# Rotary embedding: the swap of 32-row halves by transfers inside SBUF instead of a permutation matmul

## The chip, the cores and the metric

The kernel runs on one core of one Trainium2 chip. The metric is the device time of one execution in microseconds (us), smaller is better; for the kernel before it is the median of 3 runs. One more execution was taken by the profiler, and every row below is from it. The engines have short names: PE is TensorE's matmul, PEld its weight load, DVE VectorE, ACT ScalarE, POOL GpSimd, SP SyncE; SPq and POOLq are the issuing of DMAs by those engines.

## The reference: what is computed

Two transformer-like blocks for 512 tokens of width 1024. The change lies in the attention of the first one: 8 heads, and for each head q and k of two 64-wide components (128 columns together) and a v of 128 columns. q and k are normalised over each 64 columns and turned by the rotary embedding:

```python
def rope(t, cos, sin):
    tf = t.astype(jnp.float32)
    t1, t2 = jnp.split(tf, 2, axis=-1)
    out = jnp.concatenate([t1 * cos - t2 * sin, t2 * cos + t1 * sin], axis=-1)
    return out.astype(t.dtype)
...
        q = rope(rmsnorm(q, q_norm_gain[i]), cos, sin)
        k = rope(rmsnorm(k, k_norm_gain[i]), cos, sin)
...
        s = jnp.einsum('bqhcd,bkhcd->bhcqk', qblk, k).astype(jnp.float32) * scale
...
        p = jax.nn.softmax(s, axis=-1)
        a = p[:, :, 0] - lam * p[:, :, 1]
        return jnp.einsum('bhqk,bkhe->bqhe', a.astype(v.dtype), v)
```

## The kernel before

Everything is held transposed: features on the 128 partitions, the 512 tokens along the free axis. All weights are cut into 226 units of 128 output features (128x1024, 512 KB). A unit is loaded into one of four slots of `w_raw` by SP; ACT makes `w_hi` (L828) and `w_lo` = -`w_raw` (L829); and a transfer that adds, issued by POOL (L440), puts `w_raw` onto `w_lo`, where the low part of the split then stands. When it has landed it raises `lo_in` of the slot, and that tells SP that the slot of `w_raw` may be filled again, and PE that the unit may be multiplied. A tile of output is 24 matmuls (8 steps of high times high, low times high, high times low: L471 to L473) into one of two banks `pg`. A reader of a bank raises `pg_free`; `evacuated(engine, name)` waits for that.

Each engine has one instruction stream, and the order of the work is the order in which the code is written. In the stretch that matters a loop over `h` from 0 to 9 handles for each pass the tiles k, q and v of head h, the softmax of head g = h-1, and the weighted values and output norm of head h-2. PE's order in a pass from h = 2 to 7 is: tile k; the turn of v (L638) and scores of the first two query blocks of head g (L603, L605); weighted values of h-2 (`py`, L650); tile q; `turn(g, 0)` and `turn(g, 1)` (transposes of the probabilities `pa`, L613); `kq_sums` of k; the sum of squares of the output of head h-2 (`ssq_o`, L665); scores of blocks 2 and 3; tile v; `kq_sums` of q; `turn(g, 2)`, `turn(g, 3)`. In pass 0 there is only the work of head 0, and in pass 1 no L650 and no L665.

`kq_sums` (L616 to L622) holds two products for k or q: `block_ones` times the squares into the bank `px` (L620), and the permutation `rotate` times `kq_raw` into the bank `py` (L622), which swaps the 32-row halves of each 64 rows and turns one sign. Each is issued as one instruction and shows as two matmuls in the profile.

ACT evacuates a tile k or q in `kq_out` (L971 squares, L972 scaled copy `kq_raw`). `head_root` (L977 Ln, which reads `px` and frees it, and L979 Exp) makes the inverse root `kq_rs`. ACT runs in its written order: after tile q it does `kq_out` of q, the copy of `turn(g, 0)` out of PSUM (L962), `head_root` of k, `head_root` of the output, the Exps of the softmax (L950).

DVE's order in a pass from h = 2 on is: two maxima (L1477) and `combine` of blocks 0 and 1 (L1483, L1230, L1227, the last writing `pa`); a copy; the scaling of the output `hid` by `kq_rs` (L1227); the maxima of blocks 2 and 3; `rope_step` of k; `combine` of blocks 2 and 3; `rope_step` of q; a copy of `turn(g, 3)`. `scores` wait for `roped`, `turn` waits for `combed`. `rope_step` is four operations of 128x512: `kq_raw` times cosines, `py` times sines, the sum, and the product with `kq_rs`.

SP loads units 24 and on in a loop of four (L420 to L424), each as soon as its `lo_in` says so.

Of the kernel before, what the change touches and what calls it, by code (L numbers as in the profile page):

```python
# [7 lines left out]
P = 128  # L8
T = 512
D = 1024  # L10
KT = D // P
HEADS = 8
# [14 lines left out]
RING = 4  # L27
# [5 lines left out]
ALU = mybir.AluOpType  # L33
# [99 lines left out]
def aux_order():  # L133

    x, y, s = [("stat", 1), "lam", "kt"], [], []
    for name in ("bt", ("er", 0), ("er", 1), "e", "y"):
        s += [(name, 0), (name, 1)]
    for h in range(HEADS + 2):
        g = h - 1
        if 0 <= g < HEADS:  # L140
            x.append(("vt", g))
            s += [("s", g, 0), ("s", g, 1)]
        if h >= 2:
            y.append(("pv", h - 2))
        if 0 <= g < HEADS:
            s += [("t", g, 0), ("t", g, 1)]
        if h < HEADS:
            x.append(("ssq_k", h))
            y.append(("rot_k", h))
        if h >= 2:  # L150
            x.append(("ssq_o", h - 2))
        if 0 <= g < HEADS:
            s += [("s", g, 2), ("s", g, 3)]
        if h < HEADS:
            x.append(("ssq_q", h))
            y.append(("rot_q", h))
        if 0 <= g < HEADS:
            s += [("t", g, 2), ("t", g, 3)]
    x += [("stat", 2), ("stat", 3)]
    for t in range(LRU_T):  # L160
        x.append(("rg", t))
        y.append(("ig", t))
    for j in range(PAIRS + 1):
        if j > 0:
            for i in (0, 2):
                s += [("p", j - 1, i), ("p", j - 1, i + 1), ("t2", j - 1, i), ("t2", j - 1, i + 1)]
            y.append(("pv2", j - 1))
        if j < PAIRS:
            x.append(("vt2", j))
    x += [("stat", n) for n in (4, 5, 6)]  # L170
    return x, y, s
# [8 lines left out]
def build(nc, weights, x_dram, consts, rope, masks, params, ssm_b, ssm_c, lru_w, out):  # L180
    with ExitStack() as ctx:
        def sb(name, shape, dt=F32, scope=ctx):
            return scope.enter_context(nc.sbuf_tensor(name, shape, dt))

        def sem(name):
            return ctx.enter_context(nc.semaphore(name))
# [18 lines left out]
        with ExitStack() as first:  # L205
            gates = sb("gates", [P, 16, T], scope=first)
            y5 = sb("y5", [P, SSM_T, T], scope=first)
            with ExitStack() as s:
                gt = sb("gt", [P, 2, LANE_T, STEP + 1, GRP], scope=s)
                toep = sb("toep", [P, 2 * LANE_T, P], scope=s)  # L210
                e_sb = sb("e_sb", [P, 2, LANE_T, P], scope=s)
                lane = sb("lane", [P, 24, LANE_T], scope=s)
                pw = sb("pw", [P, 2, STEP + 1, LANE_T], scope=s)
                m16 = sb("m16", [P, GRP], scope=s)
                skip = sb("skip", [P, SSM_T, GRP], scope=s)
            with ExitStack() as s:
                rtab = sb("rtab", [P, 2, T], scope=s)
                kq_raw = sb("kq_raw", [P, 2, T], scope=s)
                kq_rs = sb("kq_rs", [P, 3, T], scope=s)
                rope_a = sb("rope_a", [P, 2, T], scope=s)  # L220
                kk = sb("kk", [P, 2, T], scope=s)
                qq = sb("qq", [P, 2, T], scope=s)
                v_raw = sb("v_raw", [P, T], scope=s)
                vv = sb("vv", [P, 2, QB, P], scope=s)
                pr = sb("pr", [P, 2, 2, T], scope=s)
                pa = sb("pa", [P, 2, T], scope=s)
                pt = sb("pt", [P, QB, T], scope=s)
                soft = sb("soft", [P, 2, 8], scope=s)
            mix_hi = sb("mix_hi", [P, KT, T], F32R, scope=first)
            mix_lo = sb("mix_lo", [P, KT, T], F32R, scope=first)  # L230
# [85 lines left out]
            sem(n) for n in ("e_made", "g_made", "scanned", "states", "toep_zero", "kt_made"))  # L316
        u_out, u_in, k_out, k_in, y_out, y_in = (sem(n) for n in ("u_out", "u_in", "k_out", "k_in", "y_out", "y_in"))
        gelu_done = sem("gelu_done")
        act_c, dve_c = sem("act_c"), sem("dve_c")
        roped, maxed, combed, o_sq, o_done = (sem(n) for n in ("roped", "maxed", "combed", "o_sq", "o_done"))  # L320
        rs_k, rs_q, rs_o = sem("rs_k"), sem("rs_q"), sem("rs_o")
# [30 lines left out]
        def py_read(eng, name):  # L352
            eng.wait_ge(py_free, YUSE[name] + 1)
# [13 lines left out]
        def _(sp):  # L367
# [14 lines left out]
            def next_weights(u):  # L382
                sp.wait_ge(lo_in[u % RING], 16 * (u // RING))
                sp.dma_start(w_raw[:, u % RING], weights[u].rearrange("p (k m) -> p k m", k=KT))\
                    .then_inc(w_landed[u % RING], 16)
# [30 lines left out]

            for u in range(22, 24):
                next_weights(u)
            full = len(UNITS) // RING
            with sp.Fori(24 // RING, full) as r:  # L420
                for s in range(RING):

                    sp.wait_ge(lo_in[s], r * 16)
                    sp.dma_start(w_raw[:, s], weights[r * RING + s].rearrange("p (k m) -> p k m", k=KT))\  # L424
                        .then_inc(w_landed[s], 16)
            for u in range(full * RING, len(UNITS)):
                next_weights(u)
            for k in range(KT):

                sp.wait_ge(fin_pool if k % 2 else fin_done, k // 2 + 1)  # L430
                sp.dma_start(out[:, k], hid[:, k]).then_inc(stored, 16)
# [25 lines left out]
        def _(pe):  # L457
# [30 lines left out]
            def y_use(name):  # L488
                if YUSE[name] > 0:
                    pe.wait_ge(py_free, YUSE[name])  # L490
# [125 lines left out]
            def kq_sums(h, name, n):  # L616

                x_use(("ssq_" + name, h))
                evacuated(pe, (name, h))
                pe.matmul(px[:], block_ones, kq_sq[n], start=True, stop=True).then_inc(px_full, 1)  # L620
                y_use(("rot_" + name, h))
                pe.matmul(py[:], rotate, kq_raw[:, n], start=True, stop=True).then_inc(py_full, 1)  # L622

            def glu(m):
                tile(UNIT[("glu", m // 2)], TILE[("glu", m)], XH, XL, first_split=SPLIT["g"] if m == 0 else None,
# [576 lines left out]
        def _(dve):  # L1202
# [8 lines left out]
            def link(ins):  # L1211

                put(ins, dve_c)
# [9 lines left out]
            def tt_(out_, a, b, op=ALU.mult):  # L1223
                return dve.tensor_tensor(out_, a, b, op)  # L1224
# [272 lines left out]

            def rope_step(h, name, n, ready, dst):
                evacuated(dve, (name, h))
                tt_(rope_a[:, 0], kq_raw[:, n], rtab[:, 0])  # L1500
                dve.wait_ge(py_full, YUSE[("rot_" + name, h)] + 1)
                tt_(rope_a[:, 1], py[:], rtab[:, 1]).then_inc(py_free, 1)
                py_read(dve, ("rot_" + name, h))
                link(tt_(rope_a[:, 0], rope_a[:, 0], rope_a[:, 1], ALU.add))
                dve.wait_ge(ready, h + 1)
                put(tt_(dst[:, h % 2], rope_a[:, 0], kq_rs[:, n]), roped)

            dve.wait_ge(r_landed, 16)
            for h in range(HEADS + 2):
                g = h - 1  # L1510
                attends = 0 <= g < HEADS
                if attends:
                    maximum(("s", g, 0), P, 0, soft)
                    maximum(("s", g, 1), 2 * P, 1, soft)
                    combine(g, 0)
                    combine(g, 1)
                if h == HEADS:
                    for t in range(SSM_T):
                        split_lo(SPLIT["g"] + t, x_lo[:, t], y5[:, t], x_hi[:, t])
                if h == HEADS + 1:  # L1520

                    for m in range(SSM_T):
                        evacuated(dve, ("glu", m))
                        put(tt_(y5[:, m], y5[:, m], sqr[:, m % 2]), src_done)
                    for m in range(SSM_T):
                        split_lo(SPLIT["s"] + m, x_lo[:, 4 + m], y5[:, m], x_hi[:, 4 + m])
                if attends:
                    turned(g, 1)
                if h >= 2:
                    py_read(dve, ("pv", h - 2))  # L1530
                    dve.wait_ge(rs_o, h - 1)
                    put(stt(hid[:, h - 2], hid[:, h - 2], lam_t[:, 6:7], kq_rs[:, 2]), o_done)
                if attends:
                    maximum(("s", g, 2), 3 * P, 2, soft)
                    maximum(("s", g, 3), 4 * P, 3, soft)
                if h < HEADS:
                    rope_step(h, "k", 0, rs_k, kk)
                if attends:
                    combine(g, 2)
                    combine(g, 3)  # L1540
                if h < HEADS:
                    rope_step(h, "q", 1, rs_q, qq)
                if attends:
                    turned(g, 3)
# [307 lines left out]
```

## Time and profile before

| what | value |
|---|---|
| time, median of 3 runs (lowest, highest) | 1555.84 us (1555.11, 1560.37) |
| the profiled execution's own time | 1564.44 us |
| its span, first to last instruction | 1562.6 us |
| PE busy, DVE busy, ACT busy | 94%, 41%, 53% |
| mean granted clock of TensorE | 0.969 |
| the passes h = 0 to 9, from the first `kq_raw` on | 228.0 to about 477 us |

The span leaves out 1.8 us of launch and end. Busy shares are means over stages with different limits, and a busy PE is not a PE at its peak; what a change in one stage is worth must be read from that stage's own waits. Clock is a share of full speed: 1.00 is 2.4 GHz, 0.50 is 1.2 GHz.

### The profile page before, as it was taken

The page shows a single profiled execution, that of the slowest core. Times are in us where ns is not written, and L with a number is a line of the kernel's source. Part 1 is how long each engine was busy: PE and PEld are TensorE (multiplying, and loading weights), DVE is VectorE, ACT ScalarE, POOL GpSimd, SP SyncE. Part 2 cuts the span into 40 slices and gives each one's busy share as a digit, 9 for nine tenths or more (in the row PEclk, how much of TensorE's full clock was granted, in tenths as well). Part 3 has the DMA queues.
Part 4 walks back from the last instruction along what each step waited for, and adds up shares of the span by engine and source line. Part 5 has one row for each costly group of instructions (what it writes and reads, how often), then busy time and mean ns, then how long its engine had stood idle before and what let it go on. Part 6 is the DMA issues. An engine that isn't in the chain of part 4 may idle for free.

```text
span 1562.6 us, 18066 instructions
## 1 busy us (share of the span) xinstructions
PE 1465.7 (94%) x6650; PEld 1140.8 (73%) x6654; DVE 636.1 (41%) x1116; ACT 825.3 (53%) x1147; POOL 203.7 (13%) x235
## 2 busy tenths in 40 slices
PE   4988879999989999999999999999989999999994
PEld 2876757666657887888888887677766888888883
DVE  4874004455464344555415424656515210212124
ACT  5632055666665456666535546655557554535431
POOL 0111001000001111111111111111010111111111
PEclk9998589999999999999999999999999999999997
DMA  7996276435426987888888888655484898888861
GB/s 242 189 184 116 48 186 151 108 95 118 108 61 158 243 186 167 193 191 195 194 197 182 204 195 215 157 132 126 102 183 101 194 196 187 189 196 192 193 150 57
DMA packets 82402, 253.22 MB, mean 162 GB/s; under 512 B 19856, under 2 KB 21008, under 8 KB 82192
## 3 DMA queue, kind: packets, MB, share of 16 engines
q0 software_dynamic: 32544, 118.50, 41.4%
q1 hardware_dynamic: 49344, 130.47, 28.5%
q10 hardware_dynamic: 432, 3.15, 0.6%
q8 instruction: 53, 0.87, 0.2%
q14 instruction: 29, 0.24, 0.1%
HBM read 129.14 MB, written 4.46 MB: 85 GB/s over the span
## 4 chain that ended last, share of the span: by engine, by line
PE 84%; DVE 5%; DMA 5%; ACT 2%; SPq 1%; issue 1%; POOLq 0%; POOL 0%; DVEq 0%; ACTq 0%
PE pg L471 24%; PE pg L473 24%; PE pg L472 24%; PE ps L603 1%; PE py L650 1%; PE ps L581 1%; PE ps L576 1%; DMA w_lo<-w_raw 1%; DMA w_raw<-weights 1%; PE py L622 1%; PE px L620 1%; DMA pairs<-u_dram 1%; DVE x_lo L1224 1%; DMA k_dram<-rstd 1%; PE ps L727 1%
## 5 line engine op out<-in xcount | busy, mean ns | idle before, releaser
L471 PE MATMUL pg<-x_hi,w_hi 128*128 128x512 f32 x1232 | 496.5, 403 | 21.7 <-DVE x_lo L1224 10.6
L472 PE MATMUL pg<-x_lo,w_hi 128*128 128x512 f32 x1232 | 483.8, 393 | 0.0
L473 PE MATMUL pg<-x_hi,w_lo 128*128 128x512 f32 x1232 | 483.7, 393 | 0.0
L440 POOL DMA_DIRECT2D w_lo<-w_raw x226 | 195.0, 867 | 1308.2 <-ACT w_lo L829 1281.4
L828 ACT ACTIVATE w_hi<-w_raw 128x1024 fp32r<-128x1024 f32 x226 | 237.5, 1051 | 146.9 <-PE pg L473 107.5
L471 PEld LDWEIGHTS pg<-x_hi,w_hi 128*128 128x128 f32 x1232 | 233.9, 190 | 84.0 <-issue 20.4
L472 PEld LDWEIGHTS pg<-x_lo,w_hi 128*128 128x128 f32 x1232 | 234.3, 190 | 49.8 <-issue 3.4
L473 PEld LDWEIGHTS pg<-x_hi,w_lo 128*128 128x128 f32 x1232 | 233.7, 190 | 49.9
L829 ACT ACTIVATE w_lo<-w_raw 128x1024 fp32r<-128x1024 f32 x226 | 236.4, 1046 | 0.0
L471 PE MATMUL pg<-act_hi,w_hi 128*128 128x512 f32 x432 | 170.3, 394 | 0.7 <-DMA w_lo<-w_raw 0.7
L473 PE MATMUL pg<-act_hi,w_lo 128*128 128x512 f32 x432 | 170.2, 394 | 0.0
L472 PE MATMUL pg<-act_lo,w_hi 128*128 128x512 f32 x432 | 170.2, 394 | 0.0
L471 PEld LDWEIGHTS pg<-act_hi,w_hi 128*128 128x128 f32 x432 | 80.8, 187 | 21.2 <-DMA w_lo<-w_raw 1.2
L472 PEld LDWEIGHTS pg<-act_lo,w_hi 128*128 128x128 f32 x432 | 80.8, 187 | 20.0
L473 PEld LDWEIGHTS pg<-act_hi,w_lo 128*128 128x128 f32 x432 | 80.8, 187 | 19.9
L1224 DVE TENSOR_TENSOR pairs<-rel 128x512 f32<-128x512 f32 x32 | 22.2, 692 | 150.6 <-ACT rel L1188 150.6
L1224 DVE TENSOR_TENSOR cu<-pg,rstd 128x512 f32<-128x512 f32 x44 | 30.4, 692 | 118.7 <-PE pg L473 118.6
L1227 DVE SCALAR_TENSOR_TENSOR cnv<-cu,prm,cnv 128x511 f32<-128x511 f32 x88 | 66.1, 751 | 3.1
L1224 DVE TENSOR_TENSOR hid<-hid,pg 128x512 f32<-128x512 f32 x32 | 22.0, 687 | 109.3 <-PE pg L473 109.3
L1224 DVE TENSOR_TENSOR acc<-acc,pg 128x512 f32<-128x512 f32 x24 | 16.6, 690 | 105.0 <-PE pg L473 105.0
L1477 DVE TENSOR_REDUCE soft<-ps 128x2 f32<-128x256 f32 (+3 forms) x48 | 39.6, 824 | 41.7 <-PE ps L605 35.5
L1224 DVE TENSOR_TENSOR rope_a<-kq_raw,rtab 128x512 f32<-128x512 f32 x16 | 11.1, 691 | 89.3 <-ACT kq_raw L972 88.8
(236 smaller groups left out, 1457.4 us busy)
## 6 DMA issues: line engine op xcount, KB each, us to landing
w_raw<-weights SPq DMA_DIRECT2D x226, 512.0 KB, 4.5
w_lo<-w_raw POOLq DMA_DIRECT2D x226, 512.0 KB, 5.8
hid<-x SPq DMA_DIRECT2D x4, 512.0 KB, 5.6
hid<-x ACTq DMA_DIRECT2D x1, 2048.0 KB, 12.0
out<-hid SPq DMA_DIRECT2D x8, 256.0 KB, 2.0
u_dram<-hid SPq DMA_DIRECT2D x4, 256.0 KB, 7.7
pairs<-u_dram SPq DMA_DIRECT2D x8, 128.0 KB, 10.2
y_dram<-hid SPq DMA_DIRECT2D x8, 128.0 KB, 5.0
```

The lines of the kernel that those rows point to most:

```text
L440: pool.dma_start(w_lo[:, s], w_raw[:, s], accum_op=ALU.add).then_inc(lo_in[s], 16)
L471: pe.matmul(bank[:], wh, xh(k), start=n == 0, stop=False)
L472: pe.matmul(bank[:], wh, xl(k), start=False, stop=False)
L473: last = pe.matmul(bank[:], wl, xh(k), start=False, stop=n == len(ks) - 1)
L576: pe.matmul(banks[h][:, NCH * n:NCH * n + NCH], toep[:, 2 * n + h, :], u_rows[:, 2 * n + h, :], start=True, stop=False)
L581: last = pe.matmul(banks[h][:, NCH * n + 1:NCH * n + NCH], gt[rows, r, n, 1:STEP + 1, :].rearrange("p d c -> p (d c)"), v_m[rows, r, n, 0: ...
L603: pe.matmul(bank[:, c, 0:w], qq[r, h % 2, P * i:P * i + P], kk[r, h % 2, 0:w], start=True, stop=False)
L828: act.activation(w_hi[:, s], w_raw[:, s], ACT.Copy)
L829: put(act.activation(w_lo[:, s], w_raw[:, s], ACT.Copy, scale=-1.0), hi_done)
L1224: return dve.tensor_tensor(out_, a, b, op)
L1227: return dve.scalar_tensor_tensor(out_, a, s, b, op0, op1)
L1477: put(dve.tensor_reduce(s[:, i % 2, 0:2], bank[:, :, 0:w], AX.X, ALU.max, negate=True), maxed)
```

## The change

The 16 products with `rotate` are gone. In their place SP issues, for k and for q of each head, four transfers of 32 rows by 2 KB from `kq_raw` to a new buffer `kq_rot`, each pair crossing the two 32-row halves of 64 rows. The sign moves into the table of sines `rtab`, two groups of whose rows are negated once before the loop. `rope_step` multiplies `kq_rot` by the sines in place. SP's loop over weights is written out for this stretch, so that the swaps stand at fixed places between requests for weights.

```diff
         if h < HEADS:
             x.append(("ssq_k", h))
-            y.append(("rot_k", h))
...
         if h < HEADS:
             x.append(("ssq_q", h))
-            y.append(("rot_q", h))
...
-                rope_a = sb("rope_a", [P, 2, T], scope=s)
+                rope_a = sb("rope_a", [P, T], scope=s)
+                kq_rot = sb("kq_rot", [P, 2, T], scope=s)
...
+        swapped = [sem("swapped_k"), sem("swapped_q")]
...
+            def swap_halves(h, name, n):
+
+                evacuated(sp, (name, h))
+                if h > 0:
+                    sp.wait_ge(roped, 2 * h + n - 1)
+                for b in range(0, P, 64):
+                    sp.dma_start(kq_rot[b:b + 32, n], kq_raw[b + 32:b + 64, n]).then_inc(swapped[n], 16)
+                    sp.dma_start(kq_rot[b + 32:b + 64, n], kq_raw[b:b + 32, n]).then_inc(swapped[n], 16)
+
+            ahead = 2 * RING - 2
+            for u in range(24, UNIT[("k", 0)] + ahead):
                 next_weights(u)
+            for h in range(HEADS):
+                next_weights(UNIT[("k", h)] + ahead)
+                swap_halves(h, "k", 0)
+                next_weights(UNIT[("q", h)] + ahead)
+                swap_halves(h, "q", 1)
+                next_weights(UNIT[("v", h)] + ahead)
+            weights_range(UNIT[("v", HEADS - 1)] + ahead + 1, len(UNITS))
...
-                y_use(("rot_" + name, h))
-                pe.matmul(py[:], rotate, kq_raw[:, n], start=True, stop=True).then_inc(py_full, 1)
...
             def rope_step(h, name, n, ready, dst):
                 evacuated(dve, (name, h))
-                tt_(rope_a[:, 0], kq_raw[:, n], rtab[:, 0])
-                dve.wait_ge(py_full, YUSE[("rot_" + name, h)] + 1)
-                tt_(rope_a[:, 1], py[:], rtab[:, 1]).then_inc(py_free, 1)
-                py_read(dve, ("rot_" + name, h))
-                link(tt_(rope_a[:, 0], rope_a[:, 0], rope_a[:, 1], ALU.add))
+                tt_(rope_a[:], kq_raw[:, n], rtab[:, 0])
+                dve.wait_ge(swapped[n], 64 * (h + 1))
+                link(tt_(kq_rot[:, n], kq_rot[:, n], rtab[:, 1]))
+                link(tt_(rope_a[:], rope_a[:], kq_rot[:, n], ALU.add))
                 dve.wait_ge(ready, h + 1)
-                put(tt_(dst[:, h % 2], rope_a[:, 0], kq_rs[:, n]), roped)
+                put(tt_(dst[:, h % 2], rope_a[:], kq_rs[:, n]), roped)

             dve.wait_ge(r_landed, 16)
+            ts(rtab[0:32, 1], rtab[0:32, 1], -1.0, ALU.mult)
+            link(ts(rtab[64:96, 1], rtab[64:96, 1], -1.0, ALU.mult))
```

On PE, pass 2 behind tile q, before the change (`px<-pairs,cst` at L620 is the sum of squares of k, `py<-kq_raw,cst` the rotation, L665 that of the output):

```order
767 L613 MATMUL ps<-cst,pa 128x128 [waits combed,ps_free1]
768 L613 MATMUL ps<-cst,pa 128x128
769 L620 MATMUL px<-pairs,cst 128x512 [waits pg_free0,px_free]
770 L622 MATMUL py<-kq_raw,cst 128x512 [waits py_free]
771 L665 MATMUL px<-pairs,cst 128x512 [waits o_sq,px_free]
772 L603 MATMUL ps<-kk,qq 128x384 [waits roped,ps_free0]
```

The same place after the change (L642 is the old L620, L685 the old L665, L625 the old L603):

```order
763 L635 MATMUL ps<-cst,pa 128x128 [waits combed,ps_free1]
764 L635 MATMUL ps<-cst,pa 128x128
765 L642 MATMUL px<-pairs,cst 128x512 [waits pg_free0,px_free]
766 L685 MATMUL px<-pairs,cst 128x512 [waits o_sq,px_free]
767 L625 MATMUL ps<-kk,qq 128x384 [waits roped,ps_free0]
768 L625 MATMUL ps<-kk,qq 128x384
```

The two users of `px` now stand back to back, the second with its wait for `px_free`; behind tile v in the same way `turn(g, 2)` follows the sum of squares of q directly.

On SP, from the first request behind the y transfers on, before the change (the loop over slots 0 to 3 of `w_raw`):

```order
47 L384 DMA w_raw<-weights 128x1024 [waits lo_in2]
48 L384 DMA w_raw<-weights 128x1024 [waits lo_in3]
49 L420 UNCONDITIONAL_BRANCH
50 L420 ISA
51 L424 ISA [waits lo_in0]
52 L424 DMA w_raw<-weights 128x1024
```

SP after the change, from the request for unit 26 to the swap of q of head 0 and the two requests behind it:

```order
51 L384 DMA w_raw<-weights 128x1024 [waits lo_in2]
52 L437 DMA kq_rot<-kq_raw 32x512 [waits pg_free0]
53 L438 DMA kq_rot<-kq_raw 32x512
54 L437 DMA kq_rot<-kq_raw 32x512
55 L438 DMA kq_rot<-kq_raw 32x512
56 L384 DMA w_raw<-weights 128x1024 [waits lo_in3]
57 L437 DMA kq_rot<-kq_raw 32x512 [waits pg_free1]
58 L438 DMA kq_rot<-kq_raw 32x512
59 L437 DMA kq_rot<-kq_raw 32x512
60 L438 DMA kq_rot<-kq_raw 32x512
61 L384 DMA w_raw<-weights 128x1024 [waits lo_in0]
62 L384 DMA w_raw<-weights 128x1024 [waits lo_in1]
```

Each group of four swaps now stands behind one request for weights and ahead of the next, so a swap can wait for a slot of `w_raw`, and a request for weights can wait for the evacuation of a tile.

## Rows read from the trace of the kernel before

**Rows 1.** Page, part 4: the chain that ended last, by line.
```profile
PE pg L471 24%; PE pg L473 24%; PE pg L472 24%; PE ps L603 1%; PE py L650 1%; PE ps L581 1%; PE ps L576 1%; DMA w_lo<-w_raw 1%; DMA w_raw<-weights 1%; PE py L622 1%; PE px L620 1%; DMA pairs<-u_dram 1%; DVE x_lo L1224 1%; DMA k_dram<-rstd 1%; PE ps L727 1%
```

**Rows 2.** The chain in order of time, 279 to 295 us: start, us, what.
```profile
284.89 0.76 DVE hid L1227
...
293.24 0.76 DVE pa L1227
```

**Rows 3.** Timeline, pass 4, tile k to behind tile q: start, us, work, [idle, releaser].
```profile
330.46 0.68 ACT L972 ACTIVATE kq_raw<-pg,prm 128x512 f32<-128x512 f32 x1
...
339.58 0.60 ACT L971 ACTIVATE pairs<-pg 128x512 f32<-128x512 f32 x1 [2.49 <-PE pg L473]
...
340.07 0.68 ACT L972 ACTIVATE kq_raw<-pg,prm 128x512 f32<-128x512 f32 x1
...
340.56 1.02 PE L622 MATMUL py<-kq_raw,cst 128*128 128x512 f32 x2
...
340.80 0.70 ACT L977 ACTIVATE kq_rs<-px,cst 128x512 f32<-128x512 f32 x1
...
341.55 0.30 PEld L665 LDWEIGHTS px<-pairs,cst 128*128 128x128 f32 x2 [0.79 <-ACT kq_rs L977]
```

**Rows 4.** Timeline behind tile v, the same pass.
```profile
350.97 0.62 DVE L1227 SCALAR_TENSOR_TENSOR pa<-pr,soft 128x384 f32<-128x384 f32 x1
...
351.24 1.02 PE L622 MATMUL py<-kq_raw,cst 128*128 128x512 f32 x2
...
352.10 0.49 PE L613 MATMUL ps<-cst,pa 128*128 128x128 f32 x3
...
352.59 0.75 DVE L1227 SCALAR_TENSOR_TENSOR pa<-pr,soft 128x512 f32<-128x512 f32 x1
...
353.49 0.63 PE L613 MATMUL ps<-cst,pa 128*128 128x128 f32 x4 [0.91 <-DVE pa L1227]
353.99 0.68 DVE L1224 TENSOR_TENSOR rope_a<-py,rtab 128x512 f32<-128x512 f32 x1
```

**Rows 5.** Waits, 245 to 443 us: total us, times, longest.
```profile
PE ps L613 <- DVE pa L1227: 5.4, 6, 0.9
PEld px L665 <- ACT kq_rs L977: 4.7, 6, 0.8
```

**Rows 6.** Timeline of passes 0 and 1.
```profile
245.46 0.49 PE L603 MATMUL ps<-kk,qq 64*128 64x128 f32 x4
...
253.65 0.28 ACT L962 ACTIVATE pt<-ps 128x128 f32<-128x128 f32 x1
...
254.53 0.30 PEld L603 LDWEIGHTS ps<-kk,qq 64*128 64x128 f32 x4 [0.76 <-ACT pt L962]
...
263.62 0.75 DVE L1227 SCALAR_TENSOR_TENSOR pa<-pr,soft 128x512 f32<-128x512 f32 x1
...
264.49 0.42 PEld L613 LDWEIGHTS ps<-cst,pa 128*128 128x128 f32 x4 [0.21 <-issue]
```

**Rows 7.** SP's issues (timeline; line 424), and `hid<-y_dram`, 256 KB, to landing.
```profile
233.21 22.84 SPq L424 DMA_DIRECT2D w_raw<-weights  x5
...
332.96 23.38 SPq L424 DMA_DIRECT2D w_raw<-weights  x3
...
L424 SPq DMA_DIRECT2D w_raw<-weights x15: 332/332/333, 296.3 to 431.6; - x15
...
DMA to landing us min/median/max: 2.6/4.2/6.7
```

**Rows 8.** Stretches of PE alone: length, PE busy (x), granted clock, DMA share, GB/s.
```profile
230.00:233.00 3.00, 3.00 (x7) 0.50 0.95 180
...
445.00:451.00 6.00, 5.74 (x17) 0.50 0.27 87
...
441.57:442.48 0.91, 0.00 (x1) 1.00 1.07 207
443.55:445.26 1.71, 0.00 (x0) 0.81 0.21 38
```

More of the change, by code:

```diff
@@ L418, in _, with weights_range @@
                 next_weights(u)
[L419 to L426, printed above, removed]
-                next_weights(u)
+            def weights_range(first, end):
+                inner, outer = -(-first // RING), end // RING
+                for u in range(first, inner * RING):
+                    next_weights(u)
+                with sp.Fori(inner, outer) as r:
+                    for s in range(RING):
+                        sp.wait_ge(lo_in[s], r * 16)
+                        sp.dma_start(w_raw[:, s], weights[r * RING + s].rearrange("p (k m) -> p k m", k=KT))\
+                            .then_inc(w_landed[s], 16)
+                for u in range(outer * RING, end):
+                    next_weights(u)
+            def swap_halves(h, name, n):
[7 more added lines that the diff above has]
+            for u in range(24, UNIT[("k", 0)] + ahead):
+                next_weights(u)
+            for h in range(HEADS):
[5 more added lines that the diff above has]
+            weights_range(UNIT[("v", HEADS - 1)] + ahead + 1, len(UNITS))
             for k in range(KT):
```

## The prediction

> **What bounds the kernel now.** I read the page's chain first. It is PE nearly throughout, and the rotation, L622, has its own entry of 1% in it [rows 1]. One rotation holds PE for 0.86 us (from 351.24 to 352.10, where the next product starts) [rows 4], and there are 16, so the page seems to offer 16 x 0.86 = 13.8 us. But a chain goes back at each step to whatever ended last, even if a second thing ended a tenth of a microsecond earlier. What counts is what stands next behind the rotation. So I then read the timeline of one pass of the head loop, with the releasers in brackets, at the two places where a rotation stands.
>
> Behind tile q: ACT starts on the tile at 339.58 and goes without a pause through squares, copy, the copy of the turn, and the Ln of k, which starts at 340.80 and ends at 341.50. That Ln frees `px`, and L665, which needs it, loads its weights at 341.55, released by ACT [rows 3]. The rotation starts at 340.56 and is out of the way 0.86 later, at 341.42. PE already waits 0.13 us here, and the rotation only fills a time that ACT sets.
>
> Behind tile v: the rotation starts at 351.24, `turn(g, 2)` at 352.10, and then PE stands idle 0.91 us until DVE has written the last `pa` (352.59 + 0.75 = 353.34), and goes on at 353.49 [rows 4]. From the scaling of `hid` to that last `pa` the chain consists of DVE's pieces alone, here in pass 2 from 284.89 to 294.00, 14 pieces with 0.03 us or less between them [rows 2]; and the scaling waits for Exp and Ln behind L665. So the passes have a loop that holds no rotation: end of tile q, ACT to the Ln of k, L665, Ln and Exp of the output, DVE from `hid` through maxima, rope of k and two combines, `turn(g, 3)`, tile k, scores, values, tile q.
>
> Is it so in each pass? The waits of 245 to 443 us say it: both waits stand there six times, 5.4 us and 4.7 us in total [rows 5], once for each pass from h = 2 to 7.
>
> **The change, part by part.** *Rotations of passes 2 to 7 (12 of 16).* Each takes 0.86 us from PE. At k, L665 still starts at 341.55, and PE's wait grows from 0.13 to 0.99. At q, `turn(g, 2)` needs the `pa` that is done at 351.59, so it starts near 351.7 instead of 352.10, and `turn(g, 3)` still at 353.49. Gain 0. A bound from the other side is 12 x 0.86 = 10.3 us, if those waits were to shrink with the work; nothing in the change moves ACT or DVE there, so I take 0.
>
> *Pass 0 (2 rotations).* The one of k runs in a slow spell, with the clock at 0.50 from 230 to 233 [rows 8], and takes twice its time there. Tile v takes its place in the spell and runs slow instead, so the gain is the full-clock 0.86 and not twice that. That of q is 0.86 with tile k of pass 1 directly behind. Together 1.72.
>
> *Pass 1 (2 rotations).* There is no L665. Behind the rotation of k the scores wait for ACT's copy, 253.65 + 0.28 = 253.93; they start at 254.53 [rows 6], and could at 254.0. Gain 0.5. Everything of DVE in the pass hangs on these scores, so its last `pa` comes at 263.62 + 0.75 - 0.5 = 263.9, and `turn(g, 3)` with the delay of rows 4 (0.15) at 264.0 instead of 264.49. The rotation of q gives nothing more: still 0.5.
>
> *DVE.* `rope_step` stays four operations; the one that read `py` took 0.68 us [rows 4] and reads SBUF now, where its neighbours take 0.69. The negations of `rtab` fall in a time when DVE waits for `kq_raw`. 0.
>
> *SP and the swaps, passes 2 to 7.* A DMA issue on SP takes 0.33 us, four 1.3. No transfer inside SBUF is in the trace. The nearest is `hid<-y_dram`, 256 KB, with 2.6, 4.2 and 6.7 us to landing [rows 7]; I take 4.2 and keep both ends. `kq_raw` of q is done at 340.75 [rows 3]; 1.3 of issues and up to 6.7 bring it to 348.8, and DVE wants it at 353.99 [rows 4], 5 us later. k has more room, since tile q lies between. What hides the swap is the DVE work between; without it a swap would cost 5.5 us where a rotation cost 0.86. SP's next request for weights in this pass goes out at 332.96 [rows 7]. The copy of k ends at 331.14 [rows 3], so its four swaps are issued by 332.5, ahead of that request. 0.
>
> *Swaps of pass 0.* The swap of q stands behind the request that goes out at 233.21 [rows 7]. 1.7 us of issues (that request and four swaps) and 4.2 bring it to 239.1, three operations of DVE (2.1) to 241.2; the scores want it at 245.46 - 1.72 = 243.7 [rows 6]. With 6.7 it would be 243.7, just in time. 0, at worst some tenths.
>
> Sum: 1.72 + 0.5 = 2.2 us. The profiled execution took 1564.44 us (span 1562.6 and 1.8 around it) and would take 1562.2. It is 8.6 us above the median of the runs, and I see no reason why the gain should differ there: 1555.84 - 2.2 = 1553.6.
>
> **Rivals.** *A: PE is the bound, and all of its work counts.* 1555.84 - 13.8 = 1542.0. For it speaks PE at 94% busy and its place in the chain; against it the twelve waits of rows 5, whose releasers are on ACT and DVE. Half of it, say the k side alone coming free, would give 0.86 x 6 = 5.2 more, 1548.4, and passes the bound of 0.3%. The Trainium skill (Perfetto Trace Analysis, Identifying the Most-Contended Engine) says to find the engine with the highest occupancy and improve that one first, and by that rule the sum would be rival A's 13.8; it also says that a kernel can have regimes with different limits. The rows of this stretch speak for the second. Chance 0.12 for this and for halfway.
>
> *B, slower: TensorE's clock falls in passes where it held.* With the rotation gone, PE behind tile v is idle from about 351.24 to 351.7 and from 352.1 to 353.49, some 1.8 us of 2.3. The trace has one idle pattern of 0.91 each pass that left the clock at 1.00, and one of 0.91 and 1.71 (441.57 to 442.48, 443.55 to 445.26), in which it went to 0.50 [rows 8]. The new pattern lies between. A slow spell like that of pass 0 costs 3 x 0.50 = 1.5 us of full-clock work [rows 8]. All six passes: 9.0 - 2.2 = 6.8 slower, 1562.6. With two spells the gain is gone; with five it is slower by more than 0.3%. The Trainium skill (TensorE: Matmul & The Clock Gate, Part 1) says that half clock is the default and that activity releases it; by that rule added idle time is a risk, and the rows show both outcomes. Chance 0.10.
>
> *C: the swaps come late.* If a transfer inside SBUF beside the adding transfers took over 12 us, DVE would wait in each pass, ahead of the combines at k and ahead of the next scores at q. At 15 us at q it is 1.3 + 15 - 13.2 = 3.1 per pass, less the time that the scores have in hand. Against it: no transfer of those rows took half of that. At six passes up to 19 us, 1572. Chance 0.03.
>
> **How the numbers follow.** The forecast, a gain of 0 to 3 us, has 0.75. A measurement of this kernel can tell about 0.3%, 4.7 us, from no change; a gain of 2.2 is 0.14%. The runs of before lie within 5.3 us, and one slow spell more or less moves a run by 1.5 (by 3.0 where it is as long as the one from 445 to 451 [rows 8]), so the forecast itself can land on either side of the bound: of its 0.75, 0.08 go to faster and 0.03 to slower; of B's 0.10, 0.01 stays within the bound. Faster 0.20, same 0.65, slower 0.15. The range goes from 1553.6 down by a long slow spell that is missing (3.0) and the half way of A in part, to 1549.5, and up by no gain (2.2) and two spells of B more (3.0), to 1559.0 with a little over for the spread of the runs.
>
> **What would show it.** In the timeline of a pass from h = 2 on: the second user of `px` still released by ACT's Ln, with its wait near 1.0 us; `turn(g, 3)` still released by DVE, with an idle of 1.3 to 1.4 ahead of it; a pass still 29.7 us long. Tile v of pass 0 1.7 us earlier, the scores of pass 1 0.5 after that. DVE's product with `kq_rot` without a wait from pass 1 on. Wrong would be: passes shorter by 0.9 or 1.7 us (A); the clock at 0.50 in any stretch from 245 to 440 (B); DVE waiting for a DMA in passes 1 to 7, or SP's requests for weights later than the slots come free and PE waiting for `w_lo` (C).

## The result

The changed kernel takes 1559.6 us (median of 20 runs, 1555.6 to 1564.0), the kernel before 1557.05 us in the 20 runs beside them: a ratio of 1.0015, 95% interval 1.0008 to 1.0021. It is slower by some 2.4 us, within the bound of 0.3%, where 2.2 us less was forecast; the time lies just outside the range. In a second series, below, the same kernel stood at 1.0009 (1.0000 to 1.0018), so that the loss is small, and clear of the noise in the first series only.

The page of the changed kernel gives busy times, the transfers and the chain:

```profile
span 1558.3 us, 18005 instructions
...
PE 1453.5 (93%) x6618; PEld 1134.8 (73%) x6622; DVE 636.9 (41%) x1118; ACT 825.2 (53%) x1147; POOL 203.6 (13%) x235
...
PE 81%; DVE 8%; DMA 4%; ACT 4%; issue 1%; SPq 1%; POOLq 0%; POOL 0%; DVEq 0%; ACTq 0%
...
kq_rot<-kq_raw SPq DMA_DIRECT2D x64, 64.0 KB, 2.0
```

The 64 swaps land 2.0 us after issue in the median, half of the 4.2 that I took. The profiled execution's own time is 1560.08 us against 1564.44 before, 4.4 less, although the medians differ by 2.4 the other way. Two profiled executions of this kernel can't be subtracted as wholes: the first `kq_raw` starts at 222.57 us here and at 227.97 there, before the first swap is issued. (Of the change only the two negations of `rtab` have run by then, at 216.15 us, while DVE had nothing else to do.) So I compare the stretch of the change by itself, from the copy of k of one pass to that of the next.

**The passes from h = 2 on.** Timeline of the changed kernel behind tile q of pass 4 (start, us, work, [idle before, releaser]); it answers to [rows 3]:

```profile
335.39 1.02 PE L642 MATMUL px<-pairs,cst 128*128 128x512 f32 x2
...
336.48 0.70 ACT L997 ACTIVATE kq_rs<-px,cst 128x512 f32<-128x512 f32 x1
...
337.23 0.30 PEld L685 LDWEIGHTS px<-pairs,cst 128*128 128x128 f32 x2 [1.65 <-ACT kq_rs L997]
337.23 1.12 PE L685 MATMUL px<-pairs,cst 128*128 128x512 f32 x2 [0.82 <-ACT kq_rs L997]
```

and behind tile v, which answers to [rows 4]:

```profile
347.42 0.52 PE L635 MATMUL ps<-cst,pa 128*128 128x128 f32 x3 [0.34 <-DVE pa L1247]
...
348.27 0.75 DVE L1247 SCALAR_TENSOR_TENSOR pa<-pr,soft 128x512 f32<-128x512 f32 x1
...
349.17 0.63 PE L635 MATMUL ps<-cst,pa 128*128 128x128 f32 x4 [1.24 <-DVE pa L1247]
349.67 0.68 DVE L1244 TENSOR_TENSOR kq_rot<-kq_rot,rtab 128x512 f32<-128x512 f32 x1
```

Where the rotation was, PE now waits: for the same Ln, which ends 0.05 before PE goes on, and for the same last `pa`, 0.15 before. The product with `kq_rot` follows its neighbour without a wait. Two rows of the same timeline give the length of a pass, here the copies of k of heads 2 and 7:

```profile
266.86 0.68 ACT L992 ACTIVATE kq_raw<-pg,prm 128x512 f32<-128x512 f32 x1
...
415.18 0.68 ACT L992 ACTIVATE kq_raw<-pg,prm 128x512 f32<-128x512 f32 x1
```

(415.18 - 266.86) / 5 = 29.66 us, and 29.66 before as well (271.16 to 419.45). Twelve rotations less, nothing gained.

**Passes 0 and 1** are where the two kernels part. From the first copy of k to that of head 2 the kernel before takes 43.19 us, the changed one 44.29; forecast was 2.2 less, 41.0. This 1.1 us is all that the two profiles show of the loss; the medians differ by 2.4 (1.2 to 3.3 by the interval), and what the rest is, if it is anything, they don't say. The chain of the changed kernel through this stretch (start, us, what):

```profile
222.48 4.86 DMA w_lo<-w_raw
...
227.36 0.33 SPq L384
...
227.74 1.53 SPq L437
...
229.32 1.33 SPq L438
...
230.69 0.60 SPq L437
...
231.33 6.46 DMA kq_rot<-kq_raw
...
237.81 0.70 DVE kq_rot L1244
238.51 0.02 issue
238.54 0.70 DVE rope_a L1244
239.24 0.02 issue
239.26 0.70 DVE qq L1244
239.97 0.14 issue
240.10 0.49 PE ps L625 x4
```

It is read upward from the scores of pass 1: they wait for the rotated q, and that for the swap of q. Its four issues take 1.53, 1.33, 0.60 and 1.17 us instead of 0.33 each, and the last of the four transfers lands 6.46 us after its issue began. The issues stand behind a request for weights (L384), which waits for an adding transfer. On the timeline the wait of the scores is `[1.71 <-DVE qq L1244]`, and what follows it is in the stretches of PE (length, PE busy, granted clock, DMA share, GB/s; the share counts a transfer where it starts and so can exceed 1 in a short stretch):

```profile
238.00:240.00 2.00, 0.39 (x4) 1.00 1.11 211
240.00:242.00 2.00, 1.90 (x14) 0.96 0.95 291
242.00:244.00 2.00, 2.00 (x6) 0.50 0.86 219
244.00:246.00 2.00, 2.00 (x8) 0.68 0.47 184
```

The clock falls to 0.50 soon behind the wait, and the slow spell costs 0.08 + 1.00 + 0.64 = 1.7 us of full-clock work.

### The profile page after: what moved, and what is told of

The parts are those of the page before. It is cut to its first block, busy times and chain, and to the rows that moved or that the text cites. A ratio compares the mean times of both kernels' runs of the same rounds, so it can differ in the third digit from the quotient of the medians.

```text
span 1558.3 us, 18005 instructions
## 1 busy us (share of the span) xinstructions
PE 1453.5 (93%) x6618; PEld 1134.8 (73%) x6622; DVE 636.9 (41%) x1118; ACT 825.2 (53%) x1147; POOL 203.6 (13%) x235
## 4 chain that ended last, share of the span: by engine, by line
PE 81%; DVE 8%; DMA 4%; ACT 4%; issue 1%; SPq 1%; POOLq 0%; POOL 0%; DVEq 0%; ACTq 0%
PE pg L493 24%; PE pg L495 24%; PE pg L494 24%; PE ps L625 1%; PE ps L603 1%; PE ps L598 1%; DVE soft L1497 1%; PE py L670 1%; DMA w_raw<-weights 1%; DMA w_lo<-w_raw 1%; DVE x_lo L1244 1%; DVE rope_a L1244 1%; PE ps L747 1%; DMA k_dram<-rstd 1%; DMA toep<-k_dram 1%
## 5 line engine op out<-in xcount | busy, mean ns | idle before, releaser
L1244 DVE TENSOR_TENSOR pairs<-rel 128x512 f32<-128x512 f32 x32 | 22.1, 692 | 150.3 <-ACT rel L1208 150.3
L1244 DVE TENSOR_TENSOR cu<-pg,rstd 128x512 f32<-128x512 f32 x44 | 30.4, 692 | 118.7 <-PE pg L495 118.7
L1244 DVE TENSOR_TENSOR hid<-hid,pg 128x512 f32<-128x512 f32 x32 | 22.0, 688 | 108.6 <-PE pg L495 108.5
L1244 DVE TENSOR_TENSOR acc<-acc,pg 128x512 f32<-128x512 f32 x24 | 16.5, 689 | 105.0 <-PE pg L495 105.0
L970 ACT ACTIVATE pr<-ps,soft 128x128 f32<-128x128 f32 (+3 forms) x64 | 33.2, 524 | 22.9 <-DVE soft L1497 20.6
```

The lines of the kernel that those rows point to most:

```text
L970: ins = act.activation(dst[:, c, 0:w], bank[:, c, 0:w], ACT.Exp, bias=negmax[:, i % 2, c:c + 1], **kw)
```

## The experiments

Each kernel was timed beside the kernel before in the same series; ratios are to it. "Passes 0+1" is the time from the copy of k of head 0 to that of head 2 in the profiled execution, "a pass" the mean of the five behind it. A profile is one execution and need not be a typical one: that of e8 took 1558.5 us and is the slowest of its twelve runs, that of e9 took 1537.6 and lies 3.2 below its median. Slow spells also differ between profiles. In tile v of pass 0 there is one of about 1.6 us in the profiles of before, changed, e0, e4, e8 and e10, and none in the others, so "passes 0+1" of two rows are compared only with that in mind.

| kernel | median us | ratio (95%) | passes 0+1 | a pass |
|---|---|---|---|---|
| before | 1556.7 to 1557.7 | 1 | 43.19 | 29.66 |
| changed, again (e0) | 1558.5 | 1.0009 (1.0000 to 1.0018) | 44.35 | 29.67 |
| no rotation, no swap (e1) | 1553.7 | 0.998 (0.997 to 0.999) | 39.27 | 29.66 |
| head 0 on PE (e2) | 1557.8 | 1.0001 (0.9992 to 1.001) | 40.99 | 29.67 |
| rotations and swaps both (e3) | 1556.5 | 0.9997 (0.9988 to 1.0006) | 41.56 | 29.67 |
| e2, own bank (e4) | 1545.1 | 0.9915 (0.9902 to 0.9928) | 42.61 | 27.71 |
| before, own bank (e5) | 1551.3 | 0.9963 (0.995 to 0.9975) | 41.55 | 28.77 |
| e2, rope of k early (e6) | 1543.5 | 0.9919 (0.9905 to 0.9932) | 39.93 | 27.71 |
| e2, both moves (e7) | 1535.5 | 0.9859 (0.9845 to 0.9874) | 39.92 | 26.63 |
| changed, swaps of head 0 first (e8) | 1555.1 | 0.9983 (0.9974 to 0.9992) | 40.87 | 29.67 |
| changed, both moves (e9) | 1540.8 | 0.9895 (0.9877 to 0.9913) | 43.51 | 26.63 |
| changed, swaps of head 0 by ACT (e10) | 1559.2 | 1.001 (1.000 to 1.002) | 45.66 | 29.67 |
| e8, both moves (e11) | 1535.4 | 0.986 (0.9843 to 0.9876) | 39.76 | 26.63 |

**The changed kernel again (e0).**

> The changed kernel itself once more, beside the three below on one chip. All theories: 1.001 to 1.002 of before, near 1559.5 us. The attention passes from h = 2 on 29.7 us each; the DVE product with kq_rot of pass 0 waits for the swap some 8 us and the scores of pass 1 wait 1 to 2 us for the rotated q.

As expected: DVE's two waits for the swaps of pass 0 come to 11.0 us (10.9 in the first profile of the changed kernel), the scores of pass 1 wait 1.82 us, and the slow spell stands behind that again (clock 0.63 and 0.52 from 240 to 244).

**What is the rotation worth (e1)?** Rotation and swap are both left out; q and k come out unrotated, but the order of all other work stays.

> Leaves out the swap: no rotation on PE and no transfers; DVE multiplies kq_raw itself by the sines, so q and k come out wrong, and everything else, SP's written-out order and its waits too, is as in the changed kernel. Theory 1 (the loop from tile q over ACT, L665's successor and DVE holds no rotation, and what was lost is the late swap of pass 0): a gain of 2.2 us over before, 0.9986, 1554.9 us, with passes of 29.7 us from h = 2 on, because 12 rotations hid in waits of PE. Theory 2 (PE is the bound and the transfers eat the gain): 1557 - 13.8 = 1543 us, 0.991, and passes 1.7 us shorter. Theory 3 (SP's written-out order costs the time): slower than before here too, about 1558 to 1559.5.

```diff
-                for b in range(0, P, 64):
-                    sp.dma_start(kq_rot[b:b + 32, n], kq_raw[b + 32:b + 64, n]).then_inc(swapped[n], 16)
-                    sp.dma_start(kq_rot[b + 32:b + 64, n], kq_raw[b:b + 32, n]).then_inc(swapped[n], 16)
...
-                dve.wait_ge(swapped[n], 64 * (h + 1))
-                link(tt_(kq_rot[:, n], kq_rot[:, n], rtab[:, 1]))
+                link(tt_(kq_rot[:, n], kq_raw[:, n], rtab[:, 1]))
```

3.0 us less, not 13.8. Both waits of PE stand where they were [rows 5] and have grown (245 to 443 us: total, times, longest):

```profile
PE ps L632 <- DVE pa L1244: 10.3, 13, 1.2
PEld px L682 <- ACT kq_rs L994: 9.9, 6, 1.6
```

Passes 0 and 1 take 14.28 and 24.99 us; without a slow spell they take 16.00 and 25.56 with rotations (e3). So the rotations are worth 1.72 in pass 0 and 0.57 in pass 1, and rival A is out. The Trainium skill (Perfetto Trace Analysis, Optimization Strategy) says that in some kernels the most-contended engine changes over time, and advises to look, within such a regime, for the gaps of the engine and for the semaphore that it waits on. The two rows above are that, and they agree with it: taken for the kernel as a whole, PE's 94% promised 13.8 us, and 3.0 came.

**Where does the changed kernel lose it (e2, e3)?** In e2 head 0 keeps its rotations on PE, with an unsigned permutation.

> The changed kernel with the rotations of head 0 back on PE (an unsigned permutation, the sign stays in the table); swaps by transfer from head 1 on. Theory 1: the late swaps of pass 0 are gone; gain 0.5 us in pass 1, 1556.5 us, 0.9997, and no wait of DVE for a transfer anywhere. Theory 2b (the traffic of the swaps slows the kernel in all passes): 14 of 16 swaps are left, so still 1559 us, 1.0013. Theory 3: 1559 us as well.

```diff
+                if h == 0:
+                    y_use(("rot_" + name, h))
+                    pe.matmul(py[:], rotate, kq_raw[:, n], start=True, stop=True).then_inc(py_full, 1)
...
-                swap_halves(h, "k", 0)
+                if h > 0:
+                    swap_halves(h, "k", 0)
```

In e3 all rotations stay on PE and the swaps of heads 1 to 7 run as well.

> All 16 rotations on PE as before, and from head 1 on the swaps as well, into a buffer that nobody reads (DVE only waits for them before it ends rope_step). It prices the transfers and SP's order alone. Theory 1: 0, 1557 us, 1.0000, passes of 29.7 us. Theory 2b or 3: 1559 us or more, 1.001 to 1.002.

```diff
                 pe.matmul(px[:], block_ones, kq_sq[n], start=True, stop=True).then_inc(px_full, 1)
+                y_use(("rot_" + name, h))
+                pe.matmul(py[:], rotate, kq_raw[:, n], start=True, stop=True).then_inc(py_full, 1)
...
-                dve.wait_ge(swapped[n], 64 * (h + 1))
-                link(tt_(kq_rot[:, n], kq_rot[:, n], rtab[:, 1]))
+                tt_(rope_a[:], py[:], rtab[:, 1]).then_inc(py_free, 1)
+                py_read(dve, ("rot_" + name, h))
+                if h > 0:
+                    dve.wait_ge(swapped[n], 64 * h)
```

Both stand at the time of before. The 56 swaps from head 1 on and SP's written-out order cost nothing that can be measured, and with the swaps of pass 0 the loss is gone: in the profiles pass 1 takes 24.99 us (e2) and 25.56 (e3), against 28.37 in the changed kernel. The 0.57 that e2 should be faster than e3 does not show in the medians, which are 1.3 apart the other way.

**What would it take for the rotation to count (e4 to e7)?** If the loop over ACT's Ln and DVE's chain is what hides the rotations, easing it must make them count. First the output's sum of squares gets the bank `py`, which the rotation has left, and goes ahead of the turns, and ACT takes its root ahead of that of k (e4); the same in the kernel before, with all its rotations (e5).

> Head 0 on PE, swaps by transfer from head 1 on, and the output's sum of squares goes to the bank py, which the rotation has left, ahead of the turns in passes 2 to 7; ACT takes its root ahead of that of k. So the loop no longer goes through ACT's Ln of k. If the loop of theory 1 is what held the passes, DVE's chain starts 1.9 us earlier behind tile q and a pass takes about 27.8 us instead of 29.7: 11.3 + 0.5 us less, 1545 us, 0.9925. If passes are held by anything else (transfers, weights), nothing changes against the kernel with head 0 on PE: 1557 us.

> The kernel before, all rotations on PE, with the same move of the output's sum of squares to py, ahead of the rotation there. Control for the run above: DVE's chain starts 1.6 us earlier, but PE has only 0.13 + 0.91 us of idle time per pass to give back, so PE becomes the bound and a pass takes 28.6 us: 6.2 us less, 1551 us, 0.996. The difference to the run above, about 0.85 us per pass, is then what the rotations cost once ACT and DVE don't hide them. If rotations cost nothing whatever stands around them, both runs gain the same.

```diff
                 if h < HEADS:
                     named(("q", h), XH, XL)
...
+                if 2 <= h < HEADS:
+                    y_use(("ssq_o", h - 2))
+                    pe.wait_ge(o_sq, h - 1)
+                    pe.matmul(py[:], ones, kq_sq[2], start=True, stop=True).then_inc(py_full, 1)
                 if attends:
                     turn(g, 0)
                     turn(g, 1)
```

Then the other side of the same loop: the first three operations of the rope of k move ahead on DVE (e6), and both moves together (e7). That this needs a swap which doesn't wait for PE's place behind tile q is argued from the order alone; no run has this move with the rotations on PE.

> Head 0 on PE, swaps by transfer from head 1 on, and the first three operations of the rope of k move on DVE from behind the maxima of blocks 2 and 3 to ahead of the copy of turn(g, 1), where DVE is idle; the swap has landed by then. DVE's chain up to the last pa is 2.1 us shorter, PE's idle behind tile v goes (1.7 us), and a pass takes about 27.9 us: 10.5 + 0.5 us less, 1546 us, 0.993. If DVE's chain isn't the bound, 1557 us.

> The two moves together. PE's idle of 2.76 us per pass is all gone and PE is the bound: passes of 26.9 us, 16.5 + 0.5 us less than before, 1540 us, 0.989. If the two moves remove the same wait, no better than the better one of them, 1545 us.

```diff
+                if h < HEADS:
+                    rope_turn(h, "k", 0)
                 if attends:
                     turned(g, 1)
...
                 if h < HEADS:
-                    rope_step(h, "k", 0, rs_k, kk)
+                    rope_scale(h, 0, rs_k, kk)
```

e4 and e5 came out at their numbers (1545.1 for 1545, 1551.3 for 1551). e6 is 2.5 us and e7 4.5 us faster than expected; 1.6 us of the latter is the pass of 26.63 us instead of 26.9, and the rest lies outside those passes and was not traced. With the loop eased the rotations cost 1.06 us a pass (28.77 against 27.71; 0.85 was expected), and before they cost 0. With both moves PE has no idle time left; stretches of e7 (busy of PE, PEld, DVE, ACT, POOL, clock, DMA share, GB/s):

```profile
275.00:410.00 135.00, 135.00 (x632) 95.99 (x629) 80.81 (x157) 96.05 (x194) 12.90 (x15) 1.00 0.59 138
```

**Why were the swaps of pass 0 late (e8, e10)?**

> The changed kernel, but in pass 0 SP issues both swaps ahead of the two requests for weights that stood before and between them. If the swaps of pass 0 are late because they queue behind requests for weights on SP, they land some 5 us earlier, DVE has the rotated q before the scores of pass 1 ask for it, and the time is that of a swap without delay, 1555 us. If they are late because the adding transfers keep the DMA engines busy (0.99 in that stretch), the swap of q still lands 6 us or more after its issue, the wait of 1.7 us of the scores shrinks by less than half, and the time is 1557 to 1559 us.

```diff
+                if h == 0:
+                    swap_halves(h, "k", 0)
+                    swap_halves(h, "q", 1)
+                    next_weights(UNIT[("k", h)] + ahead)
+                    next_weights(UNIT[("q", h)] + ahead)
```

> The changed kernel, but ACT issues the swaps of head 0 itself, right behind its copy, on its own queue, which holds nothing else. Same question as the run before by another way: queueing theory: landed 3 to 4 us after the copy, 1555 us plus what the eight issues cost ACT (0.4 to 0.6 us each, on the path of the Ln of k): 1556 us. Contention theory: landed 6 us or more after issue, 1558 to 1560 us.

```diff
                 free(act.activation(kq_raw[:, n], a, ACT.Copy, scale=par(gain)), (name, h))
+                if h == 0:
+                    evacuated(act, (name, h))
+                    for b in range(0, P, 64):
+                        act.dma_start(kq_rot[b:b + 32, n], kq_raw[b + 32:b + 64, n]).then_inc(swapped[n], 16)
+                        act.dma_start(kq_rot[b + 32:b + 64, n], kq_raw[b:b + 32, n]).then_inc(swapped[n], 16)
```

In e8 DVE has the swap of q 9.7 us after its copy ended (239.19 against 229.54) instead of 11.6. In its profile the scores don't wait, no slow spell follows (clock 1.00 from 232 to 252), and the median is 2.6 us below before. This is the change with two requests moved, and it gains the 2.2 us that were forecast, within the noise. The profile without a wait owes something to luck, though: its slow spell of pass 0 had held PE up. In e11 below, with the same order of SP and no spell in pass 0, the scores do wait, 1.49 us. Like is to be compared with like: with the spell, 1.71 us (changed) became 0; without it, 3.58 (e9) became 1.49 (e11). Both say that the move is worth about 2 us, less than the 5 that were expected of it.

In e10 ACT's issues take as long as SP's did:

```profile
223.44 0.59 ACTq L998 DMA_DIRECT2D kq_rot<-kq_raw  x1
224.07 1.34 ACTq L999 DMA_DIRECT2D kq_rot<-kq_raw  x1
225.44 0.95 ACTq L998 DMA_DIRECT2D kq_rot<-kq_raw  x1
226.41 0.66 ACTq L999 DMA_DIRECT2D kq_rot<-kq_raw  x1
```

The swap of k is there 1.4 us after the last issue, and 5.1 us after its copy; on SP's queue, with issues just as long, it was there 9.3 us after. So for k most of the lateness was in the landing and not in the issues. But ACT's Ln of k now stands behind the eight issues, and PE waits for it in pass 0, which takes 20.66 us:

```profile
234.61 2.07 PE L644 MATMUL px<-pairs,cst 128*128 128x512 f32 x2 [2.88 <-ACT kq_rs L1004]
```

The median, 1559.2, is the one that the contention theory named, but for this other reason. The two theories of lateness are not told apart by e10: the issues held ACT up, and with it the adding transfers, so their load on the DMA engines was not the same. What e8, e9 and e11 show is that the place behind the requests cost about 2 us of the lateness. Why issues and landings are slow in pass 0 stays open.

**All swaps by transfer, with the moves (e9, e11).**

> Both moves, with all swaps by transfer, those of head 0 too. The late swaps of pass 0 should cost the same as in the changed kernel, some 3 to 5 us against the 1535.5 of the version with head 0 on PE: 1539 to 1540 us, and passes of 26.6 us from h = 2 on. If the two are equal, the late swaps of pass 0 cost nothing once DVE's order is eased.

> Both moves, all swaps by transfer, and in pass 0 both swaps ahead of the requests for weights. If the late swap of q of pass 0 (and the slow spell behind it) is all that the version with all swaps by transfer loses against the one with head 0 on PE, this one is at least as fast as the latter, and the two rotations of head 0 that are off PE show as up to 1.7 us more: 1534 to 1535.5 us, 0.985 to 0.986. If transfers in pass 0 cost something in another way (the requests for weights that go out later), 1538 to 1541 us.

e9 loses 5.3 us to e7 by the medians, of which its profile shows 3.6 (43.51 against 39.92), and e11, which differs from it only in SP's order in pass 0, wins them back. The first row is from e9, the second from e11, and the last shows e11's PE behind its wait (length, PE busy, granted clock, DMA share, GB/s).

```profile
240.07 0.49 PE L624 MATMUL ps<-kk,qq 64*128 64x128 f32 x4 [3.58 <-DVE qq L1250]
...
236.81 0.49 PE L630 MATMUL ps<-kk,qq 64*128 64x128 f32 x4 [1.49 <-DVE qq L1256]
...
238.00:250.00 12.00, 11.76 (x56) 1.00 0.86 207
```

So e11 still waits for its swap, without a slow spell behind it. The 1.49 us are about what the two rotations of head 0 give back (1.72), and so passes 0 and 1 of e11 are hardly shorter than those of e7 (39.76 against 39.92).

e7 and e11 are the fastest, 22 us below before; they can't be told from each other.

## Why the prediction was wrong

**What bounds the kernel: right.** The loop of ACT and DVE behind tile q set the pass, 29.66 us with and without rotations, and the page's 1% for L622 promised nothing. e1 shows it, and e4 to e7 show the loop to be the one named: each side of it eased shortens the pass by 1.95 us, about what was counted from the rows (1.9 and 1.8).

**Rotations of passes 0 to 7: right.** 1.72 + 0.5 were forecast, and 1.72 + 0.57 measured (e3 against e1); the median of e1 is 3.0 us below before.

**DVE, swaps from pass 1 on: right.** No wait, and e3 prices them at nothing, though an issue took 0.59 us and not 0.33, because no nearer row was there for a transfer inside SBUF.

**"Swaps of pass 0 ... 0, at worst some tenths": this step failed.** The landing held: 6.46 us for the last transfer of q, 6.6 at most, and by the sum with 6.7 the rotated q was to be just in time. What was mis-sized is the term "1.7 us of issues (that request and four swaps)". It took 5.1 us (227.36 to 232.50), 3.4 more. Against that the request went out 0.4 us earlier than taken, and the landing, counted from the end of the issues as in the sum, took 5.3 and not 6.7. That leaves 1.6 us too late, and the scores waited 1.71: the rotated q was ready at 239.97, 13.8 us after its copy had ended. That DVE had to wait 8.55 us for the swap of k first, which I had not reckoned, moved nothing, since it waited 2.35 us more for that of q behind it.

The 0.33 us was the price of another kind of issue. A swap takes 0.51 to 0.59 us in the quiet passes and took 0.60 to 1.53 in pass 0, 8.1 us for the eight instead of 2.6. Busy DMA engines alone are not the reason. In the same stretch the request for weights at 227.36 took its 0.33, and the four swaps of pass 1, issued from 239.19 to 241.72, took 0.51 to 0.68. The two rows are the swaps of pass 0 from the second on, and those of pass 1 (length, PE busy, granted clock, DMA share, GB/s):

```profile
223.93:232.50 8.57, 8.57 (x29) 0.80 1.03 190
239.19:241.72 2.53, 1.61 (x13) 1.00 1.00 244
```

**What hangs on a late wait.** I had the price of rival B and that of rival C apart, and not that one brings the other: an idle time in front of the scores can be followed by a slow spell. It is in the profiles of the changed kernel (1.71 us), e0 (1.82) and e9 (3.58); it is not in that of e11 (1.49), nor in those of e1, e2, e3 and e8, where the scores don't wait. The wait of 1.7, the spell of 1.7 and the slow spell in pass 0 of 1.6 make the 5.0 between e1 and the changed kernel in passes 0 and 1. The medians of e1 and e0 differ by 4.8 in the same series, but how many of the timed runs had either spell isn't known. The swaps alone don't bring the spell of pass 0: before, which has none, shows it, and e9, which has them all, doesn't.

**Rival B in its own place: out.** With 1.24 + 0.34 of idle time behind tile v the clock stayed at 1.00 in all passes from h = 2 on.

## What to carry to other kernels

The chain gives an engine all the time in which it ran, even if another engine's result was due a tenth of a microsecond later; read what releases the next instruction, and take work away in a trial (e1) before moving it elsewhere. Taking a matmul off PE pays where nothing else ends at the same time. Here the transfer in its place gave nothing where the rotation stood, and 1.06 us a pass once its bank was given to another product (e4 against e5). As much again came when DVE's rope of k was moved ahead (e7 against e4), but whether this needs the transfer was not tried. Look at the first pass of a loop by itself: here its swaps stood behind requests for weights and beside adding transfers. Price an issue from one of the same kind, and where the trace has none, say so and give it a range.

## What the runs showed of the hardware

- An issue of a 32x512 transfer inside SBUF takes SP 0.59 us, against 0.33 for a 128x1024 load from memory. In pass 0, at a DMA share of 1.03, it took 0.60 to 1.53 us, and in pass 1, at a share of 1.00, 0.51 to 0.68. On ACT (e10) it took 0.51 to 1.34 us in pass 0. Landing is 1.9, 2.0 and 6.6 us (least, median, most).
- The granted clock fell behind the wait of 1.71 us in pass 1, and stayed at 1.00 through the idle times of 0.34 and 1.24 us of each later pass up to 438 us. In e11 it stayed at 1.00 behind a wait of 1.49 us; in the kernel before it had fallen behind idle times of 0.91 and 1.71 [rows 8].
